# Turning the last down products of the first and the third FFN into seven block products that add to x

## The reference

```
def half_ffn(x, i, k):
    h = rms_norm(x, norm_g[i, 2 * k])
    return x + 0.5 * swiglu(h, ffn_w_gate[i, k], ffn_w_up[i, k], ffn_w_down[i, k])

for i in range(DEPTH):                        # DEPTH = 2
    xp = half_ffn(xp, i, 0)
    hp = rms_norm(xp, norm_g[i, 1])
    yp, _ = gmlp_mixer(hp, ...)  if i % 2 == 0  else  mla_attend(mla_project(hp, ...))
    xp = xp + yp
    xp = half_ffn(xp, i, 1)                   # the same for the samples, xs
```

## Time and profile before

| | |
|---|---|
| runs, us | 2056.41, 2056.56, 2056.94; median 2056.56 |
| the profiled execution, us | 2057.66, of which the span 2055.6 |
| granted clock of TensorE | 0.998 over the span |
| PE busy | 2030.3 us, 99% |
| VectorE, ScalarE, GpSimd busy | 78%, 54%, 18% |
| chain that ended last | PE 84%, VectorE 6%, DMA 6% |

### The profile page before, as it was taken

The page is one execution under the profiler, slowest core; times in us unless marked ns, Lnnn a source line. Parts: engine busy times, 40 slices in busy tenths (PEclk is TensorE's granted clock), DMA queues, the critical chain, the costliest instruction groups (busy, mean ns, idle before and its releaser), DMA issues.

```text
span 2055.6 us, 44289 instructions
## 1 busy us (share of the span) xinstructions
PE 2030.3 (99%) x16643; PEld 1985.0 (97%) x16643; DVE 1608.6 (78%) x2678; ACT 1116.2 (54%) x1930; POOL 366.5 (18%) x453
## 2 busy tenths in 40 slices
PE   8999999999999999999999999999999999999999
PEld 8999999999999999999999999998779999999998
DVE  7679985426467898988899898768776578989998
ACT  5446564433234665655665565546475456656555
POOL 0011111122011111111111111112333221111111
PEclk9999999999999999999999999999999999999999
DMA  5366773221214677666666667452422126676775
GB/s 186 102 158 179 189 197 117 83 102 63 103 63 124 164 184 184 184 171 163 159 182 180 179 180 186 135 149 74 124 73 83 62 62 158 181 181 181 183 177 151
DMA packets 139336, 295.69 MB, mean 144 GB/s; under 512 B 22234, under 2 KB 38178, under 8 KB 133938
## 3 DMA queue, kind: packets, MB, share of 16 engines
q1 hardware_dynamic: 102306, 227.45, 33.3%
q0 software_dynamic: 36592, 66.07, 19.2%
q10 hardware_dynamic: 288, 0.18, 0.0%
HBM read 224.57 MB, written 2.66 MB: 111 GB/s over the span
## 4 chain that ended last, share of the span: by engine, by line
PE 84%; DVE 6%; DMA 6%; issue 2%; ACT 2%; SPq 1%; POOL 0%; DVEq 0%; ACTq 0%; POOLq 0%
PE side L847 27%; PE main L798 26%; PE main L847 20%; DMA raw<-raw 2%; DMA sums_w<-raw 2%; PE side L1379 1%; DVE w_lo L2125 1%; DMA raw<-in_down_tiles 1%; PE main L1124 1%; PE main L1296 1%; PE side L1338 1%; PE side L1040 1%; PE main L1192 1%; PE main L1388 1%; DMA raw<-in_up_tiles 1%
## 5 line engine op out<-in xcount | busy, mean ns | idle before, releaser
L847 PE MATMUL side<-xw_hi,w_hi 128*128 128x260 f32 x1344 | 380.4, 283 | 2.8 <-DVE tmp_in L2274 1.0
L847 PE MATMUL side<-xw_hi,w_lo 128*128 128x260 f32 x1344 | 381.0, 284 | 0.0
L847 PE MATMUL side<-xw_lo,w_hi 128*128 128x260 f32 x1344 | 380.1, 283 | 0.0
L2125 DVE TENSOR_TENSOR w_lo<-raw,w_hi 128x512 fp32r<-128x512 f32 (+2 forms) x472 | 323.6, 686 | 32.3 <-ACT w_hi L1503 14.0
L847 PE MATMUL main<-xw_hi,w_hi 128*128 128x260 f32 x1008 | 286.1, 284 | 0.0
L847 PE MATMUL main<-xw_lo,w_hi 128*128 128x260 f32 x1008 | 284.7, 282 | 0.0
L847 PE MATMUL main<-xw_hi,w_lo 128*128 128x260 f32 x1008 | 284.6, 282 | 0.0
L847 PEld LDWEIGHTS side<-xw_hi,w_hi 128*128 128x128 f32 x1344 | 253.2, 188 | 4.8 <-DVE tmp_in L2274 1.6
L847 PEld LDWEIGHTS side<-xw_hi,w_lo 128*128 128x128 f32 x1344 | 253.2, 188 | 0.0
L847 PEld LDWEIGHTS side<-xw_lo,w_hi 128*128 128x128 f32 x1344 | 252.8, 188 | 0.0
L3067 POOL DMA_DIRECT2D sums_w<-raw x116 | 100.7, 868 | 703.0 <-DMA raw<-in_gate_tiles 306.6
(11 more groups left out here) (456 smaller groups left out, 5404.6 us busy)
## 6 DMA issues: line engine op xcount, KB each, us to landing
sums_w<-raw POOLq DMA_DIRECT2D x112, 256.0 KB, 3.3
raw<-raw POOLq DMA_DIRECT2D x112, 256.0 KB, 4.7
raw<-in_gate_tiles SPq DMA_DIRECT2D x84, 256.0 KB, 4.0
raw<-in_gate_tiles SPq DMA_DIRECT2D x42, 512.0 KB, 5.1
raw<-in_up_tiles SPq DMA_DIRECT2D x84, 256.0 KB, 4.2
raw<-in_up_tiles SPq DMA_DIRECT2D x42, 512.0 KB, 5.1
raw<-in_in_tiles SPq DMA_DIRECT2D x16, 1024.0 KB, 4.8
raw<-in_down_tiles SPq DMA_DIRECT2D x56, 256.0 KB, 4.0
```

Source lines behind the costliest of these rows:

```text
L847: mm = nc.tensor.matmul(into[j], w_tiles(w, weights_at(s, j))[:, k, :], moving[:, k, order[j], :], start=(j in (0, 1) and k == 0 and i == ...
L2125: a = nc.vector.tensor_tensor(dst, src, hi.bitcast(F32), ALU.subtract)
```

## The change

The last group of the first FFN (4 pairs) and of the third (3 pairs) become `turned_down`. Their h tiles are turned as in the groups that already are, their down products run as `fast_down` in four chunks of seven block products each, and x is ready two tiles at a time.

The work for the next norm is put between the chunks. ScalarE writes the gained tile and the square of tiles 2i-2 and 2i-1 within chunk i (`normed_tile`), the last two behind chunk 4; each square has a buffer of its own (`tile_square`). Tiles 2 to 5's squares are added by four transfers of GpSimd's queue, two into tile 0's and two into tile 1's square; VectorE adds what is left in `last_tiles`. In the last chunk ("plain") the first weights of the next stage are split, in two pieces of 1024 columns. TensorE takes the next stage's first tile with a wait for each tile of x (`tile_by_tile`), and the `rms` matmul stands before tile 7's contribution. SyncE loads the spatial weights of the gMLP behind the first FFN's last down product, after two of the gMLP's weight chunks, and `w_dkv` a little earlier; TensorE transposes the spatial weights behind the gMLP's second chunk.

```
-FIRST_GROUPS = ((3, 1, False), (4, 4, True), (4, 4, False))
+FIRST_GROUPS = ((3, 1, False), (4, 4, True), (4, 4, True))
...
+        at_ffn[2].groups = LAST_GROUPS
...
+        def tile_square(k):
+            return (square_sum[:], square[:, 1, :], square[:, 0, :], tmp_in[:, 0, :], tmp_in[:, 1, :], tmp_h[:, 0, :],
+                    tmp_h[:, 1, :], tmp_next[:, 0, :])[k]
```

SyncE:

```
+            load(n, 0, in_tiles[n_u], KD, at_gmlp.lo - 6)
+            load(n + 1, 1, in_tiles[n_u + 1], KD, at_gmlp.lo - 1)
+            sp.wait_ge(tile_done, at_gmlp.tile)
+            sp.dma_start(ws_nat, gmlp_w_s[0].rearrange("g i j -> i g j")).then_inc(ws_in, 16)
...
-            load(n, 0, dq_tiles, KD, at_mla.lo - 1)
-            sp.wait_ge(lo_done, at_mla.lo)
+            load(n, 0, dq_tiles, KD, at_mla.lo - 6)
+            sp.wait_ge(lo_done, at_mla.lo - 1)
```

TensorE:

```
+            def tile_by_tile(at):
+                before = {k: lambda k=k: pe.wait_ge(xg_lo_done, at.xg + k + 1) for k in range(KD - 1)}
+                def last_x():
+                    pe.wait_ge(xg_lo_done, at.xg + KD)
+                    rms(at)()
+                before[KD - 1] = last_x
...
             v_chunk(0, 0, True)
+            v_chunk(0, 1)
             pe.wait_ge(ws_masked, 1)
...
-            out_tile(0, 0, KD, xg_hi, xg_lo, free=e - 1, before={KD - 2: last_x})
+            out_tile(0, 0, KD, xg_hi, xg_lo, free=e - 1, before=tile_by_tile(at_mla))
```

ScalarE:

```
                 elif after == "plain":
                     nc.scalar.activation(w_block(w_hi, 0, 2), raw[:, 1 - s, 0:2 * BL], ACT.Copy).then_inc(hi_done, 1)
+                    if 3 in steps:
+                        steps[3]()
...
                     nc.scalar.activation(w_block(w_hi, 2, tail), raw[:, 1 - s, 2 * BL:(2 + tail) * BL], ACT.Copy).then_inc(hi_done, 1)
+                    if 4 in steps:
+                        steps[4]()
...
+            def normed_tile(at, k, e, ro):
+                act.wait_ge(row_set, ro)
+                if k % 2:
+                    act.wait_ge(evac_done, e)
+                if k == KD - 1:
+                    tile_squares(at, k)
+                    tile_gained(at, k)
+                else:
+                    tile_gained(at, k)
+                    tile_squares(at, k)
...
+                            if in_x and not final and i:
+                                steps = {3: lambda i=i, e=e, ro=ro: normed_tile(after, 2 * i - 2, e + 4 * i, ro + i),
+                                         4: lambda i=i, e=e, ro=ro: normed_tile(after, 2 * i - 1, e + 4 * i, ro + i)}
```

VectorE, in `fast_down` and behind it:

```
+                elif at:
+                    norm_tile(at.norm, 2, at.xh)
+                    norm_tile(at.norm, 3, at.xh)
+                    dve.wait_ge(hi_done, l + 6)
+                    take_rest(w_block(w_lo, 0, 2), raw[:, 1 - s, 0:2 * BL], w_block(w_hi, 0, 2), lo_done)
...
+                elif at:
+                    dve.wait_ge(hi_done, l + 7)
+                    take_rest(w_block(w_lo, 2, 2), raw[:, 1 - s, 2 * BL:4 * BL], w_block(w_hi, 2, 2), lo_done)
+                    norm_tile(at.norm, 4, at.xh)
                 dve.wait_ge(tile_done, t + 6)
                 nc.vector.scalar_tensor_tensor(x0[:, high], other, 0.5, x0[:, high], ALU.mult, ALU.add).then_inc(evac_done, 1)
...
+            def last_tiles(at):
+                last = tile_square(KD - 1)
+                norm_tile(at.norm, 5, at.xh)
+                norm_tile(at.norm, KD - 2, at.xh)
...
+                dve.wait_ge(tile_added[0], tiles_before(at) + 32)
+                nc.vector.tensor_tensor(square_sum[:], square_sum[:], tile_square(KD - 2), ALU.add).then_inc(sum_done, KD - 2)
...
+                dve.wait_ge(tile_added[1], tiles_before(at) + 32)
+                nc.vector.tensor_tensor(last, last, tile_square(1), ALU.add).then_inc(sum_done, 1)
...
+                nc.vector.tensor_tensor(square_sum[:], square_sum[:], last, ALU.add).then_inc(sum_done, 1)
+                norm_tile(at.norm, KD - 1, at.xh)
```

GpSimd:

```
+                if at.groups[-1][2]:
+                    for k in range(2, KD - 2):
+                        pool.wait_ge(square_done, after.sums - KD + k + 1)
+                        if k >= 4:
+                            pool.wait_ge(tile_added[k % 2], tiles_before(after) + 16)
+                        pool.dma_start(tile_square(k % 2), tile_square(k), accum_op=ALU.add).then_inc(tile_added[k % 2], 16)
+                    if between:
+                        between()
```

More of the change, by code:

```diff
@@ L110, in ffn_past @@
     n, m = len(turned), len(groups) - len(turned)
-    return at.past(chunk=2 * pairs + 4 * (n + m), extra=8 * fast + 16 * n + m, tile=14 * fast + 4 * (pairs - fast) + 28 * n + 8 * m,
+    return at.past(chunk=2 * pairs + 4 * (n + m), extra=8 * fast + 16 * n + m + (groups[-1][2] and not last), tile=14 * fast + 4 * (pairs - fast) + 28 * n + 8 * m,
                    evac=8 * fast + 4 * (pairs - fast) + 16 * n + 8 * m, h=2 * pairs + 3 * n, act=2 * pairs, norm=1, rms=1,
@@ L361, in program @@
         lo_done = sem("lo_done")
+        tile_added = [sem("tile_added0"), sem("tile_added1")]
         tile_done = sem("tile_done")
@@ L625, in ffn @@
                             gate_up(i + 1, l + 10 * i + 10)
[L626 to L632, removed]
                     l += 10 * fast
@@ L995, in _ @@
             t.then_inc(ws_turned, 1)
-            v_chunk(0, 1)
             with pe.Fori(0, n_v // 2 - 1) as i:
@@ L1760, in ffn @@
                             steps = {2: sum_parts} if i == 0 else {}
+                            if in_x and not final and i:
+                                steps = {3: lambda i=i, e=e, ro=ro: normed_tile(after, 2 * i - 2, e + 4 * i, ro + i),
+                                         4: lambda i=i, e=e, ro=ro: normed_tile(after, 2 * i - 1, e + 4 * i, ro + i)}
                             fast_chunk(i % 2, 16 * ((n + i + 1) // 2 + 1), t + 7 * i, e + 4 * i, w + 2 * i,
-                                       "end" if in_x and i == 3 else "fast", raw_parts if i == 0 else None, steps,
+                                       ("end" if final else "plain") if in_x and i == 3 else "fast",
+                                       raw_parts if i == 0 else None, steps,
                                        nt=pairs, after_nt=pairs if i < 3 else 4, taken=0 if in_x and i else 2)
+                        if in_x and not final:
+                            for k in (KD - 2, KD - 1):
+                                normed_tile(after, k, e + 16, ro + 4)
                         n, t, e, w, ro, hs = n + 4, t + 28, e + 16, w + 8, ro + 4, hs + signals * pairs
@@ L2295, in fast_chunk, with fast_down @@
                     rest_third(1 - s, l + 9, after_nt)
-            def fast_down(s, raw_ready, t, e, l, w, sn, ro, i, last, own, nt):
+            def fast_down(s, raw_ready, t, e, l, w, sn, ro, i, last, own, nt, at=None):
                 low, high = slice(0, HALF), slice(HALF, TOK)
@@ L2573, in ffn @@
                                 fast_down(i % 2, 16 * ((n + i + 1) // 2 + 1), t + 7 * i, e + 4 * i, l + 5 * i, w + 2 * i, sn + 3 * i,
-                                          ro + i, i, i == 3, last_parts if i == 0 else None, pairs)
+                                          ro + i, i, i == 3, last_parts if i == 0 else None, pairs,
+                                          None if final else after)
+                                if i == 3 and not final:
+                                    last_tiles(after)
                                 continue
@@ L3106, in ffn @@
                     return
-                if after.chunk == at_ffn[2].chunk:
+                if at.groups[-1][2]:
[6 more added lines that the diff above has]
+                        between()
+                elif after.chunk == at_ffn[2].chunk:
                     add_norm_squares(after)
```

37 lines of the change are left out of this document (24 added, 13 removed).

## The result

The changed kernel takes 2062.07 us in the median of 9 runs (2059.62 to 2064.28), the kernel before 2056.61 (2055.17 to 2057.44): a ratio of 1.0025, 95% interval 1.0016 to 1.0033. It is slower by about 5 us, where 2052.2 was forecast. The profiled execution took 2060.48 us with a span of 2058.7, so it is one of the quicker ones; its span shows 3.1 us of the loss.

The account below looks back on a forecast made before the run. TensorE was taken as the bound, busy 2030.3 of 2055.6 us. First FFN -4.3 and third -0.1 gave -4.4; from 2057.66, less 1.1 for the median, that made 2052.2 us, range 2047.6 to 2056.2.

Parts of the forecast that it names:

- tail: Norm work after each new end: TensorE waits before tile 7's contribution for late squares, +0.55 us in each FFN.
- landing L: Time from issue to landing of tile 5's square-adding transfer at both new ends, taken as the median, 4.6 us.
- third rival: Squares' transfers land late beside the next stage's weight loads; at 7.9 us landing the time is 2058.8 us; chance 0.10.
- The step's own rule, L - 4.05: A landing of L us costs L - 4.05 at each tail, nothing below 4.05, 3.85 at the longest.
- waits in the group: TensorE waits for th in gate and up products, 0.6 us per middle pair: first FFN +1.2, third +0.6.
- moved loads: First FFN's last group: a wait on an adding transfer goes as spatial-weight loads move away, -0.3 us.
- first downs: Waits at the first down products for rests of turned h: third FFN +0.8 us, first FFN 0.
- last chunk, next tile's bank: TensorE waits for product 6's add to free the next tile's bank: third FFN +1.45 us, first FFN 0.
- third chunk: Third FFN's downs: a transfer into the weight sums and adds to x come late, +0.8 us.
- the twin: The fourth FFN's already turned three-pair group, used to price the third's waits; TensorE busy 31.21 of 32.22 us in its downs.
- two signs of being wrong: Third FFN keeps more than half of its 4.3 us, or the first loses more than 2.5 of its own.
- second rival: VectorE bounds the turned groups, all seven pairs costing 0.6 us instead of three: +2.4, 2054.6 us; chance 0.25.

Follow-up runs that it names:

- e2: Only the third FFN's last group turned, the first ending as before, against the kernel before: 2062.89 us, ratio 1.0031.
- e4: The changed kernel with wkv's load moved behind the landing of the squares' transfers: ratio 1.0006 to the kernel before.
- e5: The changed kernel with wkv's load moved behind the first two chunks of w_uq: ratio 0.9998 to the kernel before.
- e1: Only the first FFN's last group turned, the third ending as before, against the kernel before: 2053.68 us, ratio 0.9987.
- e10: Both FFNs turned, wkv's load behind w_uq, product 6 to x and th before rests, squares summed behind tile 7, against the kernel before: 2052.36 us, 0.9985.
- e6: Only the first FFN turned, VectorE evacuating th before the rest of two weight blocks in the up chunks, against the kernel before: 2051.20 us, 0.9979.
- e3: The changed kernel with GpSimd adding the squares of tiles 2 to 5 itself instead of four transfers: 2063.82 us, 1.0037 to the kernel before.

## Why the prediction was wrong

It was wrong at the third FFN's tail, in the landing L that it put there, and its third rival, given 0.10, named the mechanism. That rival held at one of its two places: the first FFN's last two transfers landed after 3.9 and 4.5 us. The forecast took the median landing of 4.6 us for a transfer that ran right behind a load of 1 MB. The trace of the kernel before held such cases: of the 15 transfers, the seven that took 5.5 to 7.9 us had three or more of SyncE's loads in flight beside them, and the four that had none took 3.3 to 3.6; the two loads into wkv took 7.0 in the median. The landing was 6.0 us in the changed kernel's profile and 7.6 in e2's. The step's own rule, L - 4.05, gives 1.9 and 3.55 for these; TensorE's gaps were 2.2 and 3.8. So the schedule behind the rule was right and the landing put into it was not. The prediction also drew from the Trainium skill's rule of queues served in turns ("DMA: Bandwidth & Descriptors", "Queues, rings and completion order") that the landing of a transfer beside a load stays near the median. No run here shows the packets, so nothing is said of the rule itself. The conclusion drawn from it failed: transfers of 260 KB beside the load took up to 7.6 us and without it at most 4.7 and 5.3 (e4, e5). And nothing in the prediction counted a second price of a long wait, the lower clock behind it, 2.5 us in e2.

Term by term, with gaps from the profiles, each with 0.11 us for the matmul behind it (its successor starts 0.23 us later, not 0.12), a price that was left out seven times in the third FFN:

| term, us | forecast | profile |
|---|---|---|
| first FFN, matmuls | -5.75 | -5.8 |
| waits in the group | +1.2 (two pairs) | 3 x 0.65 = +2.0 |
| moved loads | -0.3 | -0.3 |
| first downs | 0 | 0 |
| last chunk, next tile's bank | 0 | +0.35 |
| tail | +0.55 | +0.8 |
| third FFN, matmuls | -4.3 | -4.3 |
| wait in the group | +0.6 | +0.85 (0.65 in e2) |
| first downs | +0.8 | +1.3 |
| third chunk | +0.8 | +1.4 |
| last chunk, next tile's bank | +1.45 | 0.5 + 1.34 = +1.8 |
| tail | +0.55 | +2.3 here, 3.9 + 2.5 in e2 |

The first FFN's sum is then -2.95, where -4.3 was forecast and 2.7 us were gained in e1: right in sign, and about a third of it missing, half of that for the last pair, whose like in the twin doesn't wait. Of its own 5.75 us it lost more than 2.5, one of the prediction's two signs of being wrong. The third FFN's sum is +3.35 in this profile and +6.5 in e2's median, where -0.1 was forecast. Its matmuls are paid for by the waits even without the tail, +1.05 by the list. e5's profile, where the tail doesn't wait, has +1.2 (by the ratios e5 is 2.3 us behind e1); e10's, with two other waits shortened, has +0.2, about nothing gained. In the last chunk the forecast is near by its sum alone: the seventh product, said not to be held, was held for 0.4 us, and the bank made TensorE wait 1.2 and not 1.45. Of the open points, the moved transposes and spatial weights cost nothing, as said: e1's profile has no wait there. The wait of 0.3 us went with them, but that they had slowed the transfer from 304.63 on is not shown; by 304.8 all of them had landed.

VectorE as the bound in the turned groups, the second rival, held for every pair of the first FFN but the first one. It was not a lack of time but one instruction in the wrong place, as e6's profile shows.

## What to carry to other kernels

A small transfer that TensorE waits for, with no time to spare, should be priced by the landings seen beside a large load, not by the median. Where the load isn't urgent, move it, as wkv's was moved here for 4 to 5.5 us. A twin elsewhere in the kernel prices a new order well, but only for its own number of pairs, and it says nothing on what follows the end.

Fewer matmuls pay where VectorE and the transfers have slack in the same stretch: here the new order gained with products of 1.44 us (four pairs), and with 1.08 (three pairs) it lost, or about broke even once its waits were shortened.

## What was not expected of the hardware

Beside GpSimd's adds of 128 by 520, VectorE's instructions with two inputs in SBUF took up to three times their length (0.55 to 1.67 us, 0.75 to 1.78). That, with the clock behind the wait that it made, cost about as much as the transfers' late landing (1.0037 against 1.0025, with intervals that overlap).

After a wait of 3.8 us, within which it fell, TensorE's granted clock was 0.50 for 5.4 us (e2), and after one of 2.45 it averaged 0.65 over 4.7 us, beginning 1.3 us after the wait had ended; after the 2.2 us wait in the changed kernel's profile no fall shows (next 10.6 us at 1.00). The length of the wait alone doesn't tell: one of 2.0 us in e3 had a fall behind it, and one of 2.5 in e4 had none (the next 5.3 us at 1.00).
